# The delta rule's inverse on compact 64x64 squares, and taps taken between its levels

## The reference

```
q = l2norm(q) * GDN_DK ** -0.5;  k = l2norm(k);  beta = sigmoid(b)
G = cumsum(g)                                    # inside the chunk
decay = where(incl, exp(G_i - G_j), 0)
lower = where(strict, beta_i * (k k^T) * decay, 0)
sol = triangular_solve(lower + I, [v * beta, k * (beta * exp(G))])
p = (q k^T) * decay
v_new = u - w S;  o = qg S + p v_new;  S = S * gl + kg^T v_new
```

## Time and profile before

| | us |
|---|---|
| median of 3 runs | 2357.48 |
| lowest, highest | 2355.19, 2358.24 |
| the profiled execution's own time | 2354.87 |
| its span, from first to last instruction | 2352.8 |
| TensorE busy (10326 products) | 2188.8 |
| VectorE, ScalarE, GpSimd busy | 1203.7, 964.8, 777.5 |

### The profile page before, as it was taken

The page is one execution under the profiler, slowest core; times in us unless marked ns, Lnnn a source line. Parts: engine busy times, 40 slices in busy tenths (PEclk is TensorE's granted clock), DMA queues, the critical chain, the costliest instruction groups (busy, mean ns, idle before and its releaser), DMA issues.

```text
span 2352.8 us, 30345 instructions
## 1 busy us (share of the span) xinstructions
PE 2188.8 (93%) x10326; PEld 1770.9 (75%) x10326; DVE 1203.7 (51%) x1824; ACT 964.8 (41%) x1605; POOL 777.5 (33%) x336
## 2 busy tenths in 40 slices
PE   3989898998899999989979999999999989999997
PEld 2768787786678888858847888888866667888886
DVE  6476968754333332269974333323666664333322
ACT  4343453533432332265544444322455554443321
POOL 2631313311344444400004444444311104444442
PEclk8999999999999999989989999999999899999999
DMA  3310201102223233211102233322100002233322
GB/s 120 108 54 28 63 28 46 39 25 77 76 86 94 96 105 99 91 45 54 45 27 84 95 98 98 125 98 82 64 19 18 18 10 90 97 98 98 106 98 72
DMA packets 43638, 169.01 MB, mean 72 GB/s; under 512 B 4848, under 2 KB 4912, under 8 KB 43056
## 3 DMA queue, kind: packets, MB, share of 16 engines
q1 hardware_dynamic: 43056, 163.82, 21.7%
q10 hardware_dynamic: 512, 4.24, 0.5%
HBM read 165.95 MB, written 2.10 MB: 71 GB/s over the span
## 4 chain that ended last, share of the span: by engine, by line
PE 74%; DVE 13%; issue 7%; ACT 4%; POOL 1%; DMA 1%; DVEq 0%; ACTq 0%; POOLq 0%; SPq 0%
PE bank L281 20%; PE bank L282 20%; PE bank L283 20%; PE bank L777 2%; PE bank L764 2%; ACT Pr L1974 1%; POOL WL L246 1%; DVE act_q L954 1%; DVE act_v L954 1%; PE bank L1916 1%; PE bank L1419 1%; PE bank L1418 1%; PE bank L1417 1%; DVE Pr L2092 1%; PE bank L768 1%
## 5 line engine op out<-in xcount | busy, mean ns | idle before, releaser
L246 POOL TENSOR_TENSOR WL<-raw,WR 128x1024 fp32r<-128x1024 f32 (+2 forms) x274 | 712.1, 2599 | 1049.0 <-ACT WR L242 1044.3
L281 PE MATMUL bank<-XR,WR 128*128 128x512 f32 x1528 | 619.6, 405 | 30.1 <-DVE XL L426 15.0
L282 PE MATMUL bank<-XL,WR 128*128 128x512 f32 x1528 | 599.7, 392 | 0.0
L283 PE MATMUL bank<-XR,WL 128*128 128x512 f32 x1528 | 599.2, 392 | 0.0
L242 ACT ACTIVATE WR<-raw 128x1024 fp32r<-128x1024 f32 (+2 forms) x230 | 256.2, 1114 | 758.5 <-PE bank L283 750.7
L281 PEld LDWEIGHTS bank<-XR,WR 128*128 128x128 f32 x1528 | 289.8, 190 | 105.9 <-issue 30.4
L281 PE MATMUL bank<-MR,WR 128*128 128x512 f32 (+1 forms) x856 | 339.3, 396 | 16.2 <-DVE ML L1586 7.6
L282 PEld LDWEIGHTS bank<-XL,WR 128*128 128x128 f32 x1528 | 290.2, 190 | 65.7 <-issue 8.3
L283 PEld LDWEIGHTS bank<-XR,WL 128*128 128x128 f32 x1528 | 289.8, 190 | 61.7
L282 PE MATMUL bank<-ML,WR 128*128 128x512 f32 (+1 forms) x856 | 336.2, 393 | 0.0
L283 PE MATMUL bank<-MR,WL 128*128 128x512 f32 (+1 forms) x856 | 336.0, 392 | 0.0
(11 more groups left out here) (304 smaller groups left out, 2667.5 us busy)
## 6 DMA issues: line engine op xcount, KB each, us to landing
raw<-w SPq DMA_DIRECT2D x224, 512.0 KB, 3.5
raw<-w SPq DMA_DIRECT2D x48, 704.0 KB, 4.0
raw<-w SPq DMA_DIRECT2D x16, 384.0 KB, 3.0
hT<-xT SPq DMA_DIRECT2D x1, 2048.0 KB, 7.5
hT<-xT ACTq DMA_DIRECT2D x1, 2048.0 KB, 7.7
out<-Y SPq DMA_DIRECT2D x8, 256.0 KB, 2.0
memT<-memT ACTq DMA_DIRECT2D x1, 1024.0 KB, 8.1
phi<-phi ACTq DMA_DIRECT2D x1, 1024.0 KB, 6.3
```

Of the source, the lines that this page charges most:

```text
L246: nc.gpsimd.tensor_tensor(WL[:, here], raw[:, here], WR[:, here].bitcast(F32), ALU.subtract).then_inc(weight_split, 1)
L281: nc.tensor.matmul(into, wr, xr(k0 + k), start=start, stop=False)
L282: nc.tensor.matmul(into, wr, xl(k0 + k), start=False, stop=False)
L283: mm = nc.tensor.matmul(into, wl, xr(k0 + k), start=False, stop=stop)
```

## The change

A 128 x 128 lower triangular square with unit diagonal has, before the last level, nothing but two 64 x 64 squares on its diagonal. The changed kernel keeps these only: in a tile of 256 columns, 64 for each chunk, partitions 0 to 63 hold the early square of each chunk and 64 to 127 the late one. T and U of a head lie side by side in the 512 columns that T had. The masks become tables of 64 columns (six of them; the seventh 64-column table is the identity). Products of levels 0 to 4 are made for each chunk in two quarters of the array: rows and columns 0 to 63 for the early square, 64 to 127 for the late one. The late square is transposed by a plain product with the identity. Level 5 has products only for the corner below the diagonal; before it U is spread to full squares, whose upper right corner the level then fills in with -1 times its product, and whose lower left corner is cleared once at the start.

kk is made as three products of 64 x 64 for each chunk (early with early, late with late, late with early), and VectorE's and ScalarE's instructions on these tiles have 256 columns instead of 512, in level 5 on 64 partitions.

The taps of the next pair's value row of head 0 are taken out of the stretch before pT; one is issued at the end of each of the levels 0 to 3.

The last attention block's list HALF is renamed to HALVES, without any other change there; those lines are left out of the diff.

```diff
-IDENT, ONES, TRI, LEVEL0 = 0, 1, 2, 3
-N_CONST = LEVEL0 + LEVELS
+IDENT, ONES, TRI = 0, 1, 2
+N_CONST = 3
+HALF = P // 2
+N_HALF = LEVELS
+HALF_IDENT = LEVELS - 1
...
+        LAST = LEVELS - 2
+        HALVES = [slice(0, HALF), slice(HALF, P)]
+        EARLY, LATE = HALVES
+        NARROW = NB * HALF
...
+        def square_products(into, left, right):
+
+            for b in range(NB):
+                for half in HALVES:
+                    mm = nc.tensor.matmul(into[half, narrow(b)], left[half, narrow(b)], right[half, narrow(b)], start=True, stop=True)
+            return mm
+
+        def turn_squares(e, squares):
+            for b in range(NB):
+                nc.tensor.transpose(bank[6 + e][EARLY, narrow(b)], squares[EARLY, narrow(b)], ident[EARLY, EARLY])
+                mm = nc.tensor.matmul(bank[6 + e][LATE, narrow(b)], squares[LATE, narrow(b)], ident[LATE, LATE], start=True, stop=True)
+            return mm
...
-                    kb = G("keys", e)[:, of_chunk(b)]
-                    mm = nc.tensor.matmul(bank[6 + e][:, of_chunk(b)], kb, kb, start=True, stop=True)
+                    k_early, k_late = (G("keys", e)[:, of_half(b, h)] for h in BOTH)
+                    nc.tensor.matmul(bank[6 + e][EARLY, narrow(b, NARROW)], k_early, k_early, start=True, stop=True)
+                    nc.tensor.matmul(bank[6 + e][LATE, narrow(b, NARROW)], k_late, k_late, start=True, stop=True)
+                    mm = nc.tensor.matmul(bank[6 + e][LATE, narrow(b)], k_late, k_early, start=True, stop=True)
...
-                for b in range(NB):
-                    mm = nc.tensor.transpose(bank[6 + e][:, of_chunk(b)], G("T", e)[:, of_chunk(b)], ident)
-                mm.then_inc(s_["T_turned"], 1)
+                turn_squares(e, T_(e)).then_inc(s_["T_turned"], 1)
...
-                    for b in range(NB):
-                        mm = nc.tensor.matmul(bank[2 + e][:, of_chunk(b)], joins[:, of_chunk(b)], G("U", e)[:, of_chunk(b)], start=True, stop=True)
-                    mm.then_inc(s_["A_done"], 1)
-                    if lv:
+                    if lv < LAST:
+                        square_products(bank[2 + e], joins, U_(e)).then_inc(s_["A_done"], 1)
+                        if lv:
+                            turn_squares(e, U_(e)).then_inc(s_["T_done"], 1)
+                    else:
                         for b in range(NB):
-                            mm = nc.tensor.transpose(bank[6 + e][:, of_chunk(b)], G("U", e)[:, of_chunk(b)], ident)
+                            mm = nc.tensor.matmul(bank[2 + e][EARLY, narrow(b)], G("lower", e)[LATE, narrow(b)], G("U", e)[LATE, of_half(b, 1)], start=True, stop=True)
+                        mm.then_inc(s_["A_done"], 1)
+                        for b in range(NB):
+                            mm = nc.tensor.transpose(bank[6 + e][EARLY, narrow(b)], G("U", e)[EARLY, of_half(b, 0)], ident[EARLY, EARLY])
                         mm.then_inc(s_["T_done"], 1)
...
-                    for b in range(NB):
-                        mm = nc.tensor.matmul(bank[4 + e][:, of_chunk(b)], G("T", e)[:, of_chunk(b)], As[e][:, of_chunk(b)], start=True, stop=True)
-                    mm.then_inc(s_["U_done"], 1)
+                    if lv < LAST:
+                        square_products(bank[4 + e], T_(e), As[e]).then_inc(s_["U_done"], 1)
+                    else:
+                        for b in range(NB):
+                            mm = nc.tensor.matmul(bank[4 + e][EARLY, narrow(b)], T_(e)[EARLY, narrow(b)], As[e][EARLY, narrow(b)], start=True, stop=True)
+                        mm.then_inc(s_["U_done"], 1)
...
-                order.link(V.tensor_tensor(m, bank[6 + e][:, :], G("D_E", e), ALU.mult))
-                order.link(V.tensor_tensor(blocks(m), blocks(m), over_columns(row4(beta, 2 * p + e)), ALU.mult))
-                order.link(V.tensor_tensor(blocks(G("low_b", e)), blocks(m), over_blocks(const(LEVEL0)), ALU.mult))
-                V.tensor_tensor(blocks(G("T", e)), over_blocks(ident), blocks(G("low_b", e)), ALU.subtract).then_inc(s_["T_ready"], 1)
-                V.tensor_tensor(blocks(G("low_a", e)), blocks(m), over_blocks(const(LEVEL0 + 1)), ALU.mult).then_inc(s_["low_ready"], 1)
+                diagonal = m[:, NARROW:2 * NARROW]
+                V.tensor_tensor(by_chunk(diagonal[EARLY]), by_chunk(bank[6 + e][EARLY, NARROW:2 * NARROW]), by_chunk(G("D_E", e))[EARLY, :, EARLY], ALU.mult)
+                order.link(V.tensor_tensor(m[LATE].rearrange("p (q b n) -> p q b n", q=2, b=NB),
+                                           bank[6 + e][LATE, :].rearrange("p (q b n) -> p q b n", q=2, b=NB),
+                                           G("D_E", e)[LATE].rearrange("p (b q n) -> p q b n", b=NB, q=2), ALU.mult))
+                order.link(V.tensor_tensor(by_chunk(diagonal), by_chunk(diagonal), over_columns(row4(beta, 2 * p + e), HALF), ALU.mult))
+                order.link(V.tensor_tensor(by_chunk(narrow_of("low_b", e)), by_chunk(diagonal), over_half_blocks(0), ALU.mult))
+                V.tensor_tensor(by_chunk(T_(e)), over_half_blocks(HALF_IDENT), by_chunk(narrow_of("low_b", e)), ALU.subtract).then_inc(s_["T_ready"], 1)
+                V.tensor_tensor(by_chunk(narrow_of("low_a", e)), by_chunk(diagonal), over_half_blocks(1), ALU.mult).then_inc(s_["low_ready"], 1)
...
-            if not last:
-                whole(conv_steps(dve, p + 1, 1, 0))
...
+            between = iter(()) if last else conv_steps(dve, p + 1, 1, 0)
             for lv in range(LEVELS - 1):
+                rows = slice(0, P) if lv < LAST else EARLY
                 if lv:
                     dve.wait_ge(s_["T_done"], nth2(1, 5 * p + lv))
-                    V.tensor_copy(G("T", 1), bank[7][:, :]).then_inc(s_["T_moved"][1], 1)
+                    V.tensor_copy(T_(1)[rows], bank[7][rows, 0:NARROW]).then_inc(s_["T_moved"][1], 1)
                 for e in BOTH:
                     dve.wait_ge(s_["U_done"], nth2(e, 6 * p + lv + 1))
-                    V.tensor_tensor(G("U", e), G("U", e), bank[4 + e][:, :], ALU.subtract).then_inc(s_["U_moved"], 1)
-                if lv < LEVELS - 3:
+                    if lv < LAST - 1:
+                        V.tensor_tensor(U_(e), U_(e), bank[4 + e][:, 0:NARROW], ALU.subtract).then_inc(s_["U_moved"], 1)
+                    elif lv == LAST - 1:
+                        for half in HALVES:
+                            ins = V.tensor_tensor(by_chunk(G("U", e))[half, :, half], by_chunk(U_(e)[half]), by_chunk(bank[4 + e][half, 0:NARROW]), ALU.subtract)
+                        ins.then_inc(s_["U_moved"], 1)
+                    else:
+                        V.tensor_scalar(by_chunk(G("U", e))[EARLY, :, LATE], by_chunk(bank[4 + e][EARLY, 0:NARROW]), -1.0, None, ALU.mult).then_inc(s_["U_moved"], 1)
+                if lv < LAST - 2:
                     for e in BOTH:
...
+                elif lv == LAST - 2:
+                    for e in BOTH:
+                        corner = by_chunk(G("lower", e)[LATE, 0:NARROW])
+                        V.tensor_tensor(corner, corner, over_columns(row4(beta, 2 * p + e)[LATE], HALF), ALU.mult).then_inc(s_["low_ready"], 1)
+                next(between, None)
...
+            for e in BOTH:
+                order.link(nc.vector.memset(by_chunk(G("U", e))[LATE, :, EARLY], 0.0))
```

More of the change, by code:

```diff
@@ L112, in constant_tables @@
     square[:, TRI] = p <= f
-    for s in range(LEVELS):
-        square[:, LEVEL0 + s] = (p >> (s + 1) == f >> (s + 1)) & (p >> s & 1 == 1) & (f >> s & 1 == 0)
+    half = np.zeros((P, N_HALF, HALF), np.float32)
+    r, c = p % HALF, np.arange(HALF)[None, :]
+    for s in range(LEVELS - 1):
+        half[:, s] = (r >> (s + 1) == c >> (s + 1)) & (r >> s & 1 == 1) & (c >> s & 1 == 0)
+    half[:, HALF_IDENT] = r == c
     dist = SEQ - P + p - np.arange(SEQ)[None, :]
@@ L121, in constant_tables @@
     seen = np.broadcast_to(t >= L_CMP - 1, (P, NB, 1)).reshape(P, NB).astype(np.float32)
-    return np.concatenate([square.reshape(P, -1), dist, cmp.reshape(P, -1), seen], axis=1)
-TABLE_COLS = N_CONST * P + SEQ + NB * 32 + NB
+    return np.concatenate([square.reshape(P, -1), half.reshape(P, -1), dist, cmp.reshape(P, -1), seen], axis=1)
+DIST_AT = N_CONST * P + N_HALF * HALF
+TABLE_COLS = DIST_AT + SEQ + NB * 32 + NB
 TABLE_ROOM = -(-4 * TABLE_COLS // 32) * 32
@@ L166, in program @@
         ident, ones, tri = const(IDENT), const(ONES), const(TRI)
-        dist = table[:, N_CONST * P:N_CONST * P + SEQ]
-        dist_cmp = table[:, N_CONST * P + SEQ:N_CONST * P + SEQ + NB * 32]
+        dist = table[:, DIST_AT:DIST_AT + SEQ]
+        dist_cmp = table[:, DIST_AT + SEQ:DIST_AT + SEQ + NB * 32]
         seen = table[:, TABLE_COLS - NB:TABLE_COLS]
@@ L374, in over_blocks, with half_const, over_half_blocks @@
             return square.unsqueeze(1).broadcast_to([P, NB, P])
+        def half_const(i):
+            return table[:, N_CONST * P + i * HALF:N_CONST * P + (i + 1) * HALF]
+        def over_half_blocks(i):
```

(35 more changed lines are left out.)

22 lines of the change are left out of this document (11 added, 11 removed).

## The result

The changed kernel takes 2369.16 us (median of 6 runs, 2364.1 to 2377.56), the kernel before in the same comparison 2356.92 (6 runs, 2355.19 to 2358.44). The ratio is 1.0057, 95% interval 1.004 to 1.0074: about 12 us slower. Forecast was 2298, so both the sign and the size are wrong. The profiled execution took 2370.0 us with a span of 2368.0, 15.2 more than before's span; all of it is there when the delta rule ends.

A forecast was written before the change was run, and what follows sets the result against it. TensorE, 74% of the chain, was taken as the bound. Terms -41.2 (levels), -18.7 (stretch before pT and clock), -2, +0.5, +2.4 make -59.0 from 2357.5, said as 2298; range 2282 to 2350, slower case left out.

The forecast's parts named there:

- Levels: Inverse's six levels: 456 quarter passes at 27 ns, 12.3 us a pair; 17.5 us with taps, 15.5 without; gain 41.2 us.
- Added and small: kk and T's turn: 72 passes, 1.9 us against 2.7, gain 2; memsets cost 0.5, switches between whole array and parts 2.4.
- TensorE no longer sets the pace; the copies do: In the levels, VectorE's and ScalarE's copies set the length: 3.2 us for levels 1 to 3, 2.6 without tap.
- The drain that the forecast did price: TensorE switching between whole array and parts: 0.1 us, six times a pair, 2.4 us in all.
- The price of a quarter's pass: Two diagonal 64x64 quarters run side by side: 27 ns a pass taken, bounds 55 and 107; chance 0.47.
- quarters take turns: Rival for the quarter products: 55 ns a pass, levels gain only 3.6 us, total -14.2, 2343 us; chance 0.25.
- the slower rival: Rival for the quarter products: a pass stays at 107 ns, load and product in sequence; +94, 2451 us; chance 0.14.
- Taps out of the stretch before pT: VectorE's stretch ahead of the levels: waits shrink by 17.3, net 12.8, plus 5.9 of clock, together 18.7 us.
- the masks' 3.1 us: Narrower masks bring v_beta earlier on VectorE, so L744's wait on TensorE loses 3.1 us.
- collisions: GpSimd's subtraction meets VectorE's second pT mask and gate rows before the first U subtraction: 1.5 us a pair, 4.5 total.
- The gap's low clock: After TensorE's wait for pT, level 0 runs at 1.2 GHz; without the gap 5.9 us is gained.
- rival of 0.14: Clock falls to 1.2 GHz in the levels through small passes and pauses: total -10.8, 2347 us; chance 0.14.

The follow-up runs named there:

- 2307.95: Changed kernel with all turns by plain products, plus low_b's mask made behind pT and gate rows moved to the end of level 4: 2307.95 us, ratio 0.9793.
- two one-part kernels: Kernel before with only the taps moved between levels, 2335.58 us; changed kernel with only its taps put back ahead of pT, 2384.74 us.
- the taps alone: Kernel before with only the next pair's value-row taps moved to the end of levels 0 to 3, squares left whole: 2335.58 us, ratio 0.9913.
- plain-turn kernel: Changed kernel with the early square also turned by a plain product, so a turn is 16 plain passes without transposes: 2311.9 us, ratio 0.9817.
- grouped version: Changed kernel with a turn's four early transposes issued first, then the four late plain products, same twelve passes: 2342.78 us, ratio 0.9947.
- the one with both kinds in one quarter: Changed kernel with early turns before late ones, and early squares of chunks 1 and 3 turned by plain products instead of transposes: 2339.32 us, one run.
- squares alone: Changed kernel with the taps put back ahead of pT, compact squares and their turns kept: 2384.74 us, ratio 1.013 against the kernel before.

## Why the prediction was wrong

**The step that failed** is the price of a turn, in "Levels" and "Added and small": *"the late half is turned by a plain product, two passes"*, *"456, before 232. At 27 ns that is 12.3 us a pair"*, *"T's turn 12 instead of 4"*. It counted every pass of a turn at the price of a pass among its own kind, 12 x 27 ns = 0.32 us, and put a change of kind at nothing. Measured: 1.72 us with mixed kinds, 0.47 us for 16 plain passes. With it fell *"TensorE no longer sets the pace; the copies do"*: a level is 5.65 us, 5.06 of it TensorE's own passes, and was forecast at 3.2 (2.6 in pair 3). Sixteen such levels are 42 us over the forecast, and the eight turns of T ahead of them, 1.4 us over each, 11: some 53 of the 71 us between 2298 and 2369 (an estimate at full clock). No kernel of one kind alone shows it (2311.9, 2307.95), and the two one-part kernels show that the taps have no share in it. The drain that the forecast did price, 0.1 us six times a pair, was for a change of tile size; a change of kind in a quarter was not on its list. The Trainium skill (TensorEngine Tiling (Array Packing), Gotcha 2: Feature Incompatibilities) names column tiling and the transpose mode for FP32 as mutually exclusive on this chip. That could have been weighed as a warning: the early quarter's transposes do run here, but there is a pause between them and the plain products.

**The price of a quarter's pass** was right. 27 ns was taken; rows give 29 in a turn and 34 to 36 in a product with its stalls. The rival *quarters take turns* (55 ns) and the slower rival (107 ns) are refuted: the kernel did end slower, but through another mechanism, since 32 products take 1.1 us and not 3.4. Both quarters of a chunk write one PSUM bank, side by side. By the Trainium skill (TensorEngine Tiling (Array Packing), Gotcha 1: PSUM Pressure) that would not go; the measurement decides, and it goes at 29 ns a pass.

**Levels.** With one kind of turn 3.15 us, forecast 3.2 with taps. The number fits, but that is partly luck. The forecast's 3.2 was a chain of VectorE's instructions with the tap in it; in the level measured, TensorE's 88 passes fill 2.57 us and VectorE's copy of T, with the hand-overs around it, 0.59, as the chain of pair 3 above has it. The wait for T is right; the tap lies in VectorE's slack. So without taps, where 2.6 was forecast, it is 3.15 again, some 0.55 x 4 = 2 us in pair 3. In the changed kernel 5.65.

**Taps out of the stretch before pT.** Right, and sized low. Net 12.8 us of waits and 5.9 of clock were forecast, together with the narrower masks. Without the masks' 3.1 us the forecast's own terms give 15.6 (14.2 for pT, 5.9 for the clock, less 4.5 of collisions), and the taps alone brought 20.7, with v_beta's 5.9 us still there. The 4.5 us of collisions with GpSimd don't show as waits in the changed kernel (0.2 us in pair 2). They do in the plain-turn kernel, so *"What was hidden under the taps is late next"* holds once TensorE's part is short. That the longer turns and levels of the changed kernel cover them is the likely reason, not a tested one.

**The clock.** The gap's low clock went, as forecast, but the levels lowered it (rival of 0.14), with TensorE busy for 1.86 to 2.00 of each 2.00 us in the stretches shown. In pairs 0 to 2 the mean went from 0.97 or 0.98 to 0.92 or 0.93; if the clock has its two levels only, 5% of mean is 10% of 103 us at half speed, about 5 us of work a pair. The plain turns have 0.95 to 0.98 in the same stretches, with as many small passes and more; so the small passes that the rival blamed don't by themselves bring the clock down here. The grouped version has 0.96, 0.90 and 0.87, no better than the change, and is still 26 us faster: so the clock isn't the whole loss. Over the whole of the pairs (145 to 540 us; columns as the earlier trace rows) the rows of the kernel before, the change, the grouped version and the one with both kinds in one quarter are, in this order:

```profile
145.00:540.00 395.00, 366.08 (x2184) 312.49 (x2183) 295.77 (x410) 171.47 (x269) 109.29 (x59) 0.97 0.13 39
145.00:540.00 395.00, 391.24 (x3272) 314.18 (x3272) 244.65 (x406) 150.22 (x248) 107.54 (x60) 0.92 0.13 40
145.00:540.00 395.00, 377.92 (x3331) 311.13 (x3329) 265.10 (x446) 164.54 (x286) 107.88 (x60) 0.91 0.13 40
145.00:540.00 395.00, 375.75 (x3412) 304.83 (x3411) 267.25 (x453) 166.52 (x292) 108.19 (x60) 0.96 0.13 40
```

The compact kernels order themselves by the quarter transposes in a turn: with four 0.92, 0.91 and 0.90 (the change, grouped, squares alone), with two 0.96, with none 0.96, 0.95 and 0.97. The pauses don't order them: the grouped version has two changes of kind in a turn and the one with both kinds in one quarter has four, and the latter has the higher clock. By the Trainium skill (TensorE: Matmul & The Clock Gate, Part 4: PE-mode transpose) transposes don't count as busy in the same way for the clock. The order of the compact kernels agrees with it. But four whole-array transposes in a turn go with 0.97 and 0.98 (before, the taps alone), so transposes alone don't explain it either. Each of these figures is of one profiled execution, and the cause of the clock's fall stays open.

**What is left between 2298 and the plain turns' 2311.9,** 14 us. The waits for pT are 7.9 us, of which the forecast had 4.5 as collisions: 3.4 more. Pair 3's levels without taps: 2. The low clock, which the forecast had at nothing, is back behind the waits of pairs 1 and 2: 0.50 from 272 to 278 us and 0.66 from 366 to 371, at most 5 us of work by an estimate from these two stretches. The start is later: in the kernel with plain turns pair 0's first product starts at 136.2 us, in the kernel before at 133.2, 3.0 us later, where 0.5 was forecast. In the changed kernel TensorE is 1.5 us later already at the first product of the sums (18.67 against 17.20), with the first load of x at 8.12 against 7.48 us; 0.66 us is the memset of U's squares, which comes behind that product. Together at most 13 of the 14 us. Why the start is late beyond the memset stays open.

## What to carry to other kernels

When a small product is added beside another, count the changes of kind (transpose and plain product) and not just the passes: in 64x64 quarters each pair of changes cost as much as some twelve passes (0.43 us for three passes, which at 29 ns are 0.09). In quarters, turn small squares with plain products against the identity if anything near them is a plain product, and write the two quarters in turn. With the whole array there is no such pause, and a plain product only adds a pass. When work moves from one stage into another, look at what sets the pace there: the taps cost nothing in levels where VectorE had slack. And expect that a stage made shorter brings back the wait that the move had removed.

## What the runs showed of the hardware

- In 64x64 quarters a plain product starts 0.17 us after the transpose ahead of it, and a transpose 0.26 us after the start of the two-pass product ahead of it, in one quarter or in two. Plain passes in a row start 55 to 58 ns apart in one quarter and 29 ns apart in alternating ones. With the whole array the same mixture goes on at 0.11 us a pass, as without it. The Trainium skill (TensorEngine Tiling (Array Packing), Key Properties) speaks of a drain when the tiling mode changes; here the tile size stays the same and the kind changes.
- Passes of two quarters run at the same instants (464.64, 464.70) even where a row of one quarter's passes stands ahead of the other's in the program, but only some three passes deep.
- The granted clock fell with TensorE hardly idle, after quarter passes with transposes among them: 1.00 (398 to 400 us, busy for 1.86 of 2.00), 0.72 on average (408 to 410, busy for 2.00 of 2.00), 0.50 (416 to 424, busy for 7.84 of 8.00).

Not tried: a turn in which the late quarters, too, are turned by transposes, and no plain product stands among them.
